# Moving the latent half of an output projection into the steps of the differential attention

## The reference, cut to what matters

```python
mod = cond @ w_ada[0] + b_ada[0]               # adaLN: shift, scale, gate
h = rmsnorm(x) * (1 + scale) + shift
z = h @ w_in                                   # q, k, v of A; latents and rotary key of B; gate path
o_a = rmsnorm_per_head(diff_attention(...))    # A: 8 heads, softmax(q1 k1) - lam * softmax(q2 k2)
o_b = latent_attention(...) @ w_uv             # B: 8 heads
o = concat([o_a, o_b]) * silu(gate)            # 2048 wide: 1024 from A, 1024 from B
x = x + gate * (o @ w_out)                     # the output projection, 2048 x 2048
```

## Time and profile before

| what | value |
|---|---|
| three runs, median (lowest to highest) | 2091.11 us (2088.5 to 2091.54) |
| the profiled execution | 2090.51 us |
| its span | 2088.7 us |
| granted TensorE clock, mean of the span | 0.928 of 2.4 GHz |
| busy: TensorE, VectorE, ScalarE, GpSimd | 1859.8 (89%), 1278.0 (61%), 406.5 (19%), 174.2 (8%) us |

### The profile page before, as it was taken

One profiled execution on the slowest core, in us unless ns is written; L12 is line 12 of the kernel. 1 busy time (PEld: TensorE's weight loads), 2 busy tenths in 40 slices (PEclk: granted clock), 3 DMA queues, 4 the chain that ended last, 5 costly groups with the idle time before them and its releaser, 6 DMA issues.

```text
span 2088.7 us, 32490 instructions
## 1 busy us (share of the span) xinstructions
PE 1859.8 (89%) x13182; PEld 1707.9 (82%) x13182; DVE 1278.0 (61%) x1598; ACT 406.5 (19%) x863; POOL 174.2 (8%) x101
## 2 busy tenths in 40 slices
PE   4539999999999978997767799987999999999995
PEld 0109999999999966776655599987999999999995
DVE  4898677677877653553455678887334444583444
ACT  1241000000000112332344421113111111131111
POOL 2770000000600000000000011110000000001110
PEclk8879999999999999998666799997999999999997
DMA  9565555445655432116221064431322333452222
GB/s 390 219 230 186 200 196 213 183 187 209 238 201 209 162 106 61 56 32 197 73 61 57 26 287 173 182 127 56 118 102 107 105 124 112 160 192 98 80 80 85
DMA packets 77395, 307.05 MB, mean 147 GB/s; under 512 B 11416, under 2 KB 19784, under 8 KB 49440
## 3 DMA queue, kind: packets, MB, share of 16 engines
q1 hardware_dynamic: 55792, 218.56, 28.6%
q10 hardware_dynamic: 20912, 86.71, 11.6%
q0 software_dynamic: 640, 1.10, 0.1%
HBM read 278.10 MB, written 28.24 MB: 147 GB/s over the span
## 4 chain that ended last, share of the span: by engine, by line
PE 74%; DVE 14%; ACT 4%; DMA 3%; issue 2%; POOL 2%; DVEq 0%; SPq 0%; ACTq 0%; POOLq 0%
PE banks L646 73%; DVE banks L1433 2%; POOL ssq L609 2%; DMA w_more<-in_w_ada_pe 1%; ACT pxd L1241 1%; DMA d_raw<-pool_d_scratch 1%; DVE std L1660 1%; DVE w_lo L1396 1%; DVE h_lo L378 1%; DMA w_adr<-in_w_ada_dve 1%; DVE rstd L1375 1%; DVE x L1854 1%; DVE ptd_lo L1709 0%; ACT px L1185 0%; DVE pt_lo L1602 0%
## 5 line engine op out<-in xcount | busy, mean ns | idle before, releaser
L646 PE MATMUL banks<-h_hi,w_hi 128*128 128x272 f32 x3712 | 774.4, 290 | 36.2 <-DVE h_lo L1414 15.1
L646 PE MATMUL banks<-h_hi,w_lo 128*128 128x272 f32 x3712 | 772.7, 290 | 0.0
L646 PE MATMUL banks<-h_lo,w_hi 128*128 128x272 f32 x3712 | 770.1, 289 | 0.0
L646 PEld LDWEIGHTS banks<-h_hi,w_hi 128*128 128x128 f32 x3712 | 588.0, 190 | 41.6 <-issue 19.0
L646 PEld LDWEIGHTS banks<-h_lo,w_hi 128*128 128x128 f32 x3712 | 588.0, 190 | 0.0
L646 PEld LDWEIGHTS banks<-h_hi,w_lo 128*128 128x128 f32 x3712 | 584.4, 190 | 0.0
L1433 DVE CUSTOM_DVE_ANT_0 banks<-w_adr,cond_b 128x2048 f32<-128x2048 f32 x160 | 387.0, 2419 | 18.9 <-DMA w_adr<-in_w_ada_dve 15.7
L1396 DVE TENSOR_TENSOR w_lo<-w_raw,w_hi 128x2048 fp32r<-128x2048 f32 x117 | 299.4, 2559 | 4.0
L1395 DVE CAST w_hi<-w_raw 128x2048 fp32r<-128x2048 f32 x117 | 145.2, 1241 | 225.1 <-PE banks L646 216.9
L634 POOL TENSOR_TENSOR ssq<-ssq,stage 128x544 f32<-128x544 f32 x32 | 48.1, 1502 | 1261.3 <-ACT stage L1054 1261.3
L1131 ACT ACTIVATE stage<-banks 128x544 f32<-128x544 f32 x48 | 30.2, 628 | 519.4 <-PE banks L646 519.4
(11 more groups left out here) (288 smaller groups left out, 1675.9 us busy)
## 6 DMA issues: line engine op xcount, KB each, us to landing
w_adr<-in_w_ada_dve ACTq DMA_DIRECT2D x60, 1024.0 KB, 4.9
w_raw<-in_w_z SPq DMA_DIRECT2D x32, 1024.0 KB, 6.2
w_raw<-in_w_pin SPq DMA_DIRECT2D x32, 1024.0 KB, 4.8
w_adr<-in_w_ada_dve SPq DMA_DIRECT2D x20, 1024.0 KB, 4.9
w_raw<-in_w_gate SPq DMA_DIRECT2D x16, 1024.0 KB, 6.1
w_raw<-in_w_out SPq DMA_DIRECT2D x16, 1024.0 KB, 4.9
w_raw<-in_w_pout SPq DMA_DIRECT2D x16, 1024.0 KB, 4.8
w_more<-in_w_ada_pe SPq DMA_DIRECT2D x10, 1024.0 KB, 7.2
```

The costliest lines, as they stand in the source:

```text
L646: return pe.matmul(out, lhsT, rhs, start=start, stop=stop)
```

## The change

The output projection is cut in two halves over its input features. The latent half (input tiles 8 to 15, 48 matmuls for an output tile) is computed before the diff half (tiles 0 to 7). Weights are loaded, rounded and subtracted by halves of 1024 columns; the rounding moves from VectorE to ScalarE. The first 13 output tiles of the latent half lie in steps 0 to 38 of the differential attention, as the last thing of a step, three, three and two input tiles (18, 18 and 12 matmuls); the tiles 13, 14 and 15 lie around the norm. Each finished tile is evicted by ScalarE scaled by the gate, added by GpSimd to a tile of x from HBM, and stored to a scratch tensor in HBM, from which x is loaded at the output stage. For this, banks 6 and 7 are freed: all transposes and value products of the attention now alternate between banks 4 and 5 in the order of `d_jobs`, and the value products come ahead of the step's transposes. The loads of the condition vector and of the first adaLN tiles no longer wait for the last head. Memory is laid out anew so that the new tiles fit. Semaphores of the latent attention's sample part are merged with others.

The diff, cut to its core:

```diff
+        d_jobs = []
+        for w in range(D_UNITS + DLAG + 1):
+            if w > DLAG and (w - DLAG - 1) % 9 == 8:
+                d_jobs.append(("s", (w - DLAG - 1) // 9))
+            d_jobs += [("v", h) for h in range(HEADS) if w == v_step(h)]
+            d_jobs += [("o", h) for h in range(HEADS) if w == d_last(h) + DLAG + 1]
+            if DLAG <= w < D_UNITS + DLAG:
+                d_jobs.append(("t", w - DLAG))
+                if (w - DLAG) % 9 == 8:
+                    d_jobs.append(("r", w - DLAG))
+        chunk_of = ((0, 1, 2), (3, 4, 5), (6, 7))
+        IN_STEPS = 13
...
@@ SP: loads in the steps of the attention, then behind it
+            def load_half(src, g):
+                sp.wait_ge(split_ready, g - G_KPE)
+                sp.dma_start(w_raw[:, g % 2, 0:D // 2], src).then_inc(raw_in[g % 2], 16)
+            def load_x_half(n):
+                if n >= 2:
+                    sp.wait_ge(x1_out[n % 2], 16 * (n // 2))
+                sp.dma_start(x_half[n % 2][:], xT[:, n]).then_inc(x1_in[n % 2], 16)
...
+                if w % 3 == 1 or w == 0:
+                    load_half(w_out[(w + 8) // 3][:, D // 2:D], G_OUT + (w + 8) // 3)
+                if w % 3 == 2 and w > 2:
+                    load_x_half((w + 1) // 3)
+            sp.wait_ge(df_pv, HEADS)
             sp.dma_start(sgd[:], g_scr[0:HEADS].rearrange("h p r -> p h r")).then_inc(df_g_in, 16)
+            for n in range(14, KT):
+                load_x_half(n)
+            sp.wait_ge(dfs_od, HEADS // 2)
             sp.dma_start(sel_row[:], selr).then_inc(df_r_in, 16)
-            sp.wait_ge(df_fin, HEADS)
             sp.dma_start(cond_b[:], cB.to_broadcast((P, 2 * D)).rearrange("p (a d) -> p a d", a=2)).then_inc(condb_in, 16)
             for s in range(2):
                 load_ada(s, w_ada_dve[ADA_P0 + ADA_P1 + s])
+            for s in range(2):
+                load_half(w_out[s][:, 0:D // 2], G_O2 + s)
+            for s in range(2):
+                sp.wait_ge(x1_out[s], 16 * 6)
+            sp.dma_start(x[:, 0:12], x1_scr[0:12].rearrange("t p r -> p t r")).then_inc(x_in, 16)
...
@@ POOL
+            for n in range(KT):
+                pool.wait_ge(x1_in[n % 2], 16 * (n // 2 + 1))
+                pool.wait_ge(x1_ev, n + 1)
+                pool.tensor_tensor(x_half[n % 2][:], x_half[n % 2][:], y_half[n % 2][:], ALU.add).then_inc(x1_added, 1)
...
@@ PE
+            def latent_half(n, ks):
+                g = G_OUT + n
+                if 0 in ks:
+                    pe.wait_ge(split_ready, g - G_KPE + 2)
+                    pe.wait_ge(acc_free[(g - 1) % 2], turn_of(g + 1))
+                for k in ks:
+                    m = half_products(6, g, k, HEADS + k, k == 0, k == HEADS - 1)
+                if HEADS - 1 in ks:
+                    m.then_inc(mm_done, 1)
             for w in range(D_UNITS + DLAG + 1):
                 if w < D_UNITS:
                     d_scores(w)
+                if w > DLAG and (w - DLAG - 1) % 9 == 8:
+                    d_sample_values((w - DLAG - 1) // 9)
                 for h in range(HEADS):
                     if w == v_step(h):
                         d_values_in(h)
-                if DLAG <= w < D_UNITS + DLAG:
-                    d_turn(w - DLAG)
                 for h in range(HEADS):
                     if w == d_last(h) + DLAG + 1:
                         d_values(h)
-                if w - DLAG - 1 >= 0 and (w - DLAG - 1) % 9 == 8:
-                    d_sample_values((w - DLAG - 1) // 9)
+                if DLAG <= w < D_UNITS + DLAG:
+                    d_turn(w - DLAG)
+                if w < 3 * IN_STEPS:
+                    latent_half(w // 3, chunk_of[w % 3])
+            latent_half(13, range(HEADS))
...
+            latent_half(14, range(HEADS))
+            latent_half(15, range(4))
...
+            with pe.Fori(1, KT // 2) as t:
+                for s in range(2):
+                    diff_half(G_O2 + s, 2 * t, t)
...
@@ ACT
+            def half_hi(g, t2=0, t=0):
+                act.wait_ge(raw_in[g % 2], 16 * t + 16 * (g // 2 + 1 - ADA_PE // 2))
+                act.wait_ge(mm_done, t2 + (g - 1))
+                act.activation(half_slots(g)[0], w_raw[:, g % 2, 0:D // 2], ACT.Copy).then_inc(w_upper, 1)
...
+                if w < 3 * IN_STEPS and w % 3 == 2:
+                    if w // 3:
+                        store_half(w // 3 - 1)
+                    evict_half(w // 3)
+                if w % 3 == 0 and w and w // 3 + 1 <= IN_STEPS:
+                    half_hi(G_OUT + w // 3 + 1)
+            half_hi(G_OUT + 14)
...
             act.activation(rs8[:], rs8[:], ACT.Sqrt).then_inc(df_std, 1)
+            store_half(13)
+            evict_half(14)
+            half_hi(G_O2)
...
                     ins.then_inc(acc_free[slot], 1)
+                    if halves:
+                        half_hi(g0 + s + 2, 2 * t, t)
                     act.wait_ge(x_new, 2 * t + (KT * (n - 1) + s + 1))
                     square(2 * t + s, stage[:, s])
...
@@ DVE
+            def half_lo(g, t2=0, t=0):
+                hi, lo = half_slots(g)
+                dve.wait_ge(w_upper, t2 + (g - G_OUT + 1))
+                dve.tensor_tensor(lo, w_raw[:, g % 2, 0:D // 2], hi.bitcast(F32), ALU.subtract).then_inc(split_ready, 1)
...
+                if w % 3 == 1 and w > 3 and w // 3 + 1 <= IN_STEPS:
+                    half_lo(G_OUT + w // 3 + 1)
...
                     ada_tile(ADA_P0 + ADA_P1 + s, 2 * t, t)
-                    update(G_OUT + s, 2 * t, t, 1, s, s)
-                    split(G_OUT + s + 2, 2 * t, t)
+                    update(G_O2 + s, 2 * t, t, 1, s, s)
+                    half_lo(G_O2 + s + 2, 2 * t, t)
```

330 lines of the change are left out of this document (201 added, 129 removed).

## The result

The changed kernel takes 2124.38 us (median of 4 runs, 2118.38 to 2125.77) against 2091.32 us (4 runs, 2088.5 to 2092.87): ratio 1.0154, 95% interval 1.0132 to 1.0177. It is slower by 1.5%, on the side that was forecast, 13.5 us above the number and inside the range. The profiled execution took 2125.24 us, its span is 2123.5 us against 2088.7, so 34.8 us are to be found.

A forecast was written before the change was run, and what follows sets the result against it. It took engines waiting for each other to bound the attention, and TensorE and a VectorE-ScalarE ring, nearly equal, the projection. From 2090.5 us, attention +36.7 and behind it -16.3 (gain 23.1, cost 6.8) gave 2110.9, range 2079 to 2134.

The forecast's parts named there:

- The ring: Output stage: serial round of dot products, eviction, update, rounding, remainder on VectorE and ScalarE; 9.95 us a tile, gain 23.1 us.
- Remainders in steps 1 and 4: Attention: VectorE's 1.2 us remainder of the weight half, straight in the step's round where VectorE leads, seven times: 8.4 us.
- Step 2: Attention, k = 2 of nine: fifth transpose waits for ScalarE's eviction of the value product; 6.2 against 4.74, 4.35 us in all.
- Step 3: Attention, k = 3 of nine: sample products, transpose, chunk and scores on TensorE; 6.0 against 4.76, 3.75 us in all.
- Steps 7: Attention, k = 7 of nine: values, transposes, chunk and sample scores on TensorE; 6.8 against 6.2, 1.0 us over four groups.
- the evictions: Attention: ScalarE's evictions of the latent tile end later than the next maximum at k = 5 and k = 8: 4.7 us.
- The clock: Attention: TensorE relapses to 1.2 GHz once a group, 1 us each: 4 us.
- The norm: Between last sample product and first dot product: late weight half, then four rounds of product and widening; cost 6.8 us.
- The clock rival: Attention: TensorE stays at 1.2 GHz through most of k = 2, 3 and 7; 2149 us, chance 0.10.
- The faster one: Attention costs only 16.9 us and GpSimd's add costs the projection half as much; 2083.8 us, chance 0.16.
- The one without a change: Whole kernel: attention costs 20 us and the late weight comes on time; 2092 us, chance 0.12.
- The one that had the stage at TensorE's 6.0 a tile: Output stage falls to TensorE's matmul time and the attention's chunks hide; 2029 us, chance 0.02.

The follow-up runs named there:

- the eviction-first kernel: Changed kernel with ScalarE asking for the next adaLN tile behind the eviction and the rounding of the next weight half instead of ahead of them: 2102.3 us.
- the thin adds: Changed kernel with GpSimd's adds of half sums and of squares cut from 544 columns to 1: 2106.4 us.
- three edits on the other engines: Changed kernel with remainders in steps 2, 3 and 7, diff weight halves asked for before the last x tile, adaLN load behind the eviction: 2086.9 us.
- a fourth: On top of those three edits, the eight widenings of the reciprocal roots made of rounded halves, four fp32r matmuls a head: 2078.8 us.
- the moved remainders: Changed kernel with VectorE's remainder of the next weight half in steps 2, 3 and 7 of each group of nine instead of 1, 4 and 7: 2114.3 us.

## Why the prediction came out as it did

**The output stage was right.** The ring was forecast at 9.95 and measured at 9.84, the stage at 155.5 and 153.5. That it is a ring over two engines, not TensorE, is shown by the eviction-first kernel, and that GpSimd's add costs it 1.0, by the thin adds (1.16). The Trainium skill, page SBUF — State Buffer, section on its two separate sides, would have had an add hold the port pair to its end: that is what the negation of two elements shows (1.21 us, ended with the add), and the dot product that starts 0.4 us after its add loses 1.13. The 19 us that I worked out from it for the attention did not come: where TensorE's chunk is gone, the add costs 1.03 us in three steps 6.

**The attention was right in size and in part in place** (+40.3 from the end of the latent attention's sample part to E, forecast +36.7). Remainders in steps 1 and 4: 8.4 forecast, 8.0 measured. Step 2: 6.2 against 6.15 with the wait for ScalarE's eviction where it was put (the parts that I listed add up to 5.95, so 0.25 of the 6.2 had no source). Step 3: 6.0 against 6.15, but in the fourth group that step had been 3.82 and not 4.76, so it cost 2.3 there. Steps 0 to 2 of the first group: 2.8 against 1.9, and its step 3, which had no term, 0.9. Steps 7: 1.0 against 3.1.

Wrong in place: the evictions, put at 4.7 over steps 6 and 0 of all groups. Steps 0 did not grow at all (5.26), steps 6 grew by 7.0. Of these, 3.1 are the adds, which stay when the chunk is gone (4.60 in three groups). The other 3.9 are TensorE's chunk, which waits for the eviction and then runs at 1.2 GHz in all four groups; where it waits and then runs at 2.4 GHz the step takes 3.61, so the eviction alone costs nothing. The adds come out near my 3 in this count, but they lie beside the chunk's side of the step, and leaving them out gave nothing. The clock: 4, for one relapse a group. It fell in step 6 of every group, behind the idle time of step 5 as forecast (2.95 and 1.85 us in the third group), and once more in steps 2 and 3 of the second (7.63 and 7.66), which cost 3.0; with the 3.9 that is up to 6.9. So the sum of the attention is in part luck, errors that balance: the evictions took nothing by themselves, the clock more than its term.

**The norm was the term that failed**: "four rounds of a six-matmul product 0.75 and a widening 0.9", with the last subtraction at E + 43.3 and the first dot product at E + 49.9. Measured E + 60.7. Its weight landed at E + 34.9 instead of E + 31.5: 3.4, of which 2.2 is that its batch took 14.67 us and not the 12.5 of the earlier trace rows. From there to the first subtraction's end it was 3.0, as forecast. Then the rounds: 17.5 us from first to last subtraction instead of 8.8. The SiLU behind them cost 1.2 less than forecast. The widening was priced at 0.9 by a sum's matmuls at full clock; a row of the kernel before that I had passed over has the very operation, partly at half clock:

```profile
1195.63 11.25 PE L646 MATMUL banks<-rs,sel_row 8*128 8x272 f32 x32
```

that is 1.41 a head, and the half-clock products behind it. In the old kernel it mattered little whether that was seen; in the new one the widenings stand in the chain. At 1.2 GHz a round is 1.6 and 2.18. With 3.77 in place of 1.65 for four rounds the sum would have come to 2110.9 + 8.5 = 2119.4. The forecast allowed for relapses of the clock in the attention and for none in the norm; both had them. What lets it fall in the norm the runs do not show.

**Rivals.** The clock rival (1.2 GHz through most of steps 2, 3 and 7) did not come: 0.91 over the attention. The faster one needed the adds at half their cost and steps 2 and 3 for nothing; steps 2 and 3 cost what was forecast and more. The one without a change needed the weight on time; it landed 3.4 us behind even the forecast's. The one that had the stage at TensorE's 6.0 a tile did not come either: 9.84, with TensorE idle beside it. Of the signs named in advance, update period and clock came as said (9.84; 0.91), the attention of 209.5 us (1012.43 to E = 1221.94) is above the 200 to 207, and the first dot product missed its 50 by 10.7.

## What to carry to other kernels

Before halving an engine's work, trace the ring that runs beside it, and shorten that first or with it: here the change cost 33 us, and it took three edits on the other engines (two that only move an instruction in a queue, one that moves seven operations to other steps, of which three were hidden there) to make it worth about 5 us, and a fourth, which the kernel before could also have, to make it 13. Price an operation that moves onto the chain from its own row, at the clock level that the row shows, not from a like one. Where two waits end within a microsecond of each other, an experiment on one of them shows next to nothing; the pair has to be taken together. And an edit's gain is read step by step: of the 8.9 us of the moved remainders only 3.4 were what the edit was made for.

## What was not expected of the hardware

A VectorE operation on 128 x 2 elements, from one tile to itself, took 1.21 us beside a GpSimd add of 1.34 and 0.17 without: the length does not protect it. TensorE's clock went to 1.2 GHz in the norm with gaps of at most 1.2 us in front, where it had f32 widenings of 8 rows among its work. With the same values as fp32r halves (0.5 us a head instead of 1.05) and the weight on time the clock was 1.00 over the stretch; with the weight late it was at full speed up to a wait of 6.99 us and at 1.2 GHz behind it. What decides there stays open. So does what moves the first maximum by 4 us between profiles of the same code.
